# Two heads as one 48-row block in the recurrence, 128-row attention scores with the forget sums as a row sent by DMA, and alternating head products

## The reference

```
# branch a (rwkv): per head a 64x64 state S, over the 272 tokens
sa = S a_t
S  = S * w_t + sa b_t^T + v_t k_t^T
y_t = S r_t
# then a norm of each head, a bonus term, and a gate

# branch b (fox): q, k normed per head, c = cumsum(log_sigmoid(f)) per head
sc = q k^T / 8 + c[query] - c[key]       (causal)
out = softmax(sc) v
```

## Time and profile before

| | |
|---|---|
| median of three runs | 3304.73 us (3299.08 to 3321.63) |
| the profiled execution | 3333.08 us, its span 3331.0 us |
| mean granted TensorE clock of it | 0.955 |
| TensorE busy | 3198.3 us (96%) |
| DVE busy | 1728.7 us (52%) |
| ScalarE busy | 1240.5 us (37%) |
| HBM traffic | 145 GB/s over the span |

### The profile page before, as it was taken

How to read it: one execution, slowest core, us unless ns; L and a number is a source line. 1 busy time by engine, 2 the same in 40 slices (tenths; PEclk the granted TensorE clock), 3 DMA queues, 4 the chain that set the end, 5 groups by cost and what they waited for, 6 DMA issues and landing times.

```text
span 3331.0 us, 58202 instructions
## 1 busy us (share of the span) xinstructions
PE 3198.3 (96%) x24889; PEld 3018.6 (91%) x24889; DVE 1728.7 (52%) x2641; ACT 1240.5 (37%) x1824; POOL 61.3 (2%) x92
## 2 busy tenths in 40 slices
PE   7999889999999989979999999999999999999999
PEld 6999889999999989978878778778899999999999
DVE  5567565445554456454454444454465555555444
ACT  4354354333333444342222222333544333333343
POOL 0001000000000000000000000000000000000000
PEclk9999999999999999997897888999999999999999
DMA  5665445555555544542121111433354555555554
GB/s 199 199 170 144 137 142 177 188 180 186 187 179 188 187 154 147 174 123 55 52 68 49 45 40 52 126 102 90 122 180 167 180 186 188 180 187 183 185 188 139
DMA packets 369801, 484.93 MB, mean 146 GB/s; under 512 B 11847, under 2 KB 181142, under 8 KB 369638
## 3 DMA queue, kind: packets, MB, share of 16 engines
q1 hardware_dynamic: 362752, 471.55, 44.0%
q0 software_dynamic: 3600, 7.86, 0.8%
q10 hardware_dynamic: 3302, 3.39, 0.3%
HBM read 475.76 MB, written 7.01 MB: 145 GB/s over the span
## 4 chain that ended last, share of the span: by engine, by line
PE 89%; DVE 7%; ACT 3%; issue 1%; DMA 0%; DVEq 0%; SPq 0%; POOL 0%; ACTq 0%; POOLq 0%
PE psum L339 20%; PE psum L338 20%; PE psum L337 20%; PE psum L1683 7%; PE psum L468 5%; PE psum L472 4%; PE psum L470 4%; DVE w_lo L319 1%; DVE w_lo L455 1%; PE psum L1651 1%; ACT w_hi L310 1%; PE psum L2315 1%; DVE arena L1959 1%; PE psum L2314 1%; DVE arena L773 0%
## 5 line engine op out<-in xcount | busy, mean ns | idle before, releaser
L337 PE MATMUL psum<-act_hi,w_hi 128*128 128x256 f32 (+1 forms) x5840 | 1652.2, 283 | 61.7 <-DVE act_lo L864 18.1
L338 PE MATMUL psum<-act_lo,w_hi 128*128 128x256 f32 (+1 forms) x5840 | 1655.7, 284 | 0.0
L339 PE MATMUL psum<-act_hi,w_lo 128*128 128x256 f32 (+1 forms) x5840 | 1654.6, 283 | 0.0
L319 DVE TENSOR_TENSOR w_lo<-w_raw,w_hi 128x1024 fp32r<-128x1024 f32 x728 | 858.7, 1221 | 894.0 <-ACT w_hi L310 893.9
L310 ACT ACTIVATE w_hi<-w_raw 128x1024 fp32r<-128x1024 f32 x728 | 730.6, 1051 | 1207.6 <-PE psum L339 1207.6
L337 PEld LDWEIGHTS psum<-act_hi,w_hi 128*128 128x128 f32 x5840 | 1111.8, 190 | 68.6 <-issue 28.9
L339 PEld LDWEIGHTS psum<-act_hi,w_lo 128*128 128x128 f32 x5840 | 1113.1, 191 | 0.0
L338 PEld LDWEIGHTS psum<-act_lo,w_hi 128*128 128x128 f32 x5840 | 1104.8, 189 | 0.3
L468 PE MATMUL psum<-act_hi,w_hi 128*128 128x256 f32 (+1 forms) x1280 | 398.4, 311 | 2.5 <-DVE arena L1352 2.5
L470 PE MATMUL psum<-act_lo,w_hi 128*128 128x256 f32 (+1 forms) x1280 | 373.1, 291 | 0.0
L472 PE MATMUL psum<-act_hi,w_lo 128*128 128x256 f32 (+1 forms) x1280 | 372.8, 291 | 0.0
(11 more groups left out here) (374 smaller groups left out, 1672.1 us busy)
## 6 DMA issues: line engine op xcount, KB each, us to landing
w_raw<-w_in SPq DMA_DIRECT2D x128, 1024.0 KB, 5.5
w_raw<-w_down SPq DMA_DIRECT2D x88, 1024.0 KB, 5.1
w_raw<-w_gate_up SPq DMA_DIRECT2D x88, 1024.0 KB, 4.8
w_raw<-w_gate SPq DMA_DIRECT2D x44, 1024.0 KB, 5.0
w_raw<-w_up SPq DMA_DIRECT2D x44, 1024.0 KB, 5.1
w_raw<-w_out SPq DMA_DIRECT2D x16, 1024.0 KB, 5.2
w_raw<-w_o SPq DMA_DIRECT2D x16, 1024.0 KB, 5.1
w_raw<-w_branch_a SPq DMA_DIRECT2D x8, 1024.0 KB, 5.1
```

Of the source, the lines that this page charges most:

```text
L319: nc.vector.tensor_tensor(w_lo[:, s % 2, 2 * h:2 * h + 2, 0:wd], w_raw[:, s % RAW, 2 * h:2 * h + 2, 0:wd], w_hi[:, s % 2, 2 * h:2 * h + 2, ...
L337: pe.matmul(dst, w1, x1, start=first, stop=False, skip_group_check=True)
L338: pe.matmul(dst, w1, x0, start=False, stop=False, skip_group_check=True)
L339: mm = pe.matmul(dst, w0, x1, start=False, stop=stop and k == UNIT_K - 1, skip_group_check=True)
```

## The change

What is computed stays the same. In the recurrence, the 16-row blocks of the two heads are kept as one 48-row block (the first head in rows 0 to 15, the second in rows 32 to 47, zeros elsewhere, cleared once), and are multiplied once, with the second head's products. The three transposes of the 16 tokens become six products of 64 rows. The gram products go to other PSUM banks, DVE masks the half that the inversion needs first and the other half in two parts later, and DVE's filler slots are placed otherwise. The products x, y, state and s0 alternate between the heads.

In the attention, the q and k operands of each head have 128 rows: 64 with the head's values, one row of ones in q against the head's forget sums in k, zeros in the rest. POOL sends the forget sum rows from `c_neg` by two DMAs for each pair of heads. The scores are then one 128-row product. The products of `o` alternate between heads; the sums of squares of q and k go to two column groups of one bank, so that reciprocal, root and spread work on rows 0 to 15 and 32 to 47. The forget gate's logarithm is taken in the recurrence's groups 4 (DVE), 5 (ACT) and 6 (DVE).

```diff
+        PAIR = 32 + META
+        mh = [slice(32 * h, 32 * h + META) for h in range(2)]
...
-        tokm = place(3, P)
-        gm0 = place(2, 2 * META)
+        tokm = place(3, RHD)
+        gm0 = place(2, PAIR)
         inv_s = [place(4, P) for _ in range(6)]
-        inv_m = [place(2, META) for _ in range(6)]
+        inv_m = [place(PAIR) for _ in range(6)]
...
-                return psum[0:META, 2 * q + bank, 2 * P:2 * P + META]
-            return psum[:, 2 * (q // 2) + bank, (q % 2) * P:(q % 2 + 1) * P]
+                return psum[0:PAIR, 4 + bank, 2 * P:2 * P + PAIR]
+            return psum[:, 4 * (q // 2) + bank, (q % 2) * P:(q % 2 + 1) * P]
...
+                hs = [slice(h * RHD, (h + 1) * RHD) for h in range(2)]
                 for n, src in enumerate((bh[:, 0:META], kh[:, 0:META], zt(16 + j)[:, 0:META])):
-                    mm = pe.transpose(psum[0:META, 2, n * P:(n + 1) * P], src, ident)
+                    for h in range(2):
+                        mm = pe.matmul(psum[mh[h], 2, n * RHD:(n + 1) * RHD], src[hs[h]],
+                                       ident[hs[h], hs[h]], start=True, stop=True)
...
+                            o = psum[:, 2 * n + h, 2 * P * c:2 * P * (c + 1)].rearrange(
+                                "p (a t) -> p a t", a=2)
+                            pe.matmul(o[0:64], src[r, t0:t0 + 64], ar[r, :, t0:t0 + P],
...
-                    return f(h, True) if meta else last
+                    return f(h, True) if meta and h else last
...
-                for h in range(2):
-                    mm = pe.matmul(psum[0:META, 0, hs[h]], gm0[0:META, h, META:2 * META],
-                                   tokm[0:META, 2, hs[h]], start=True, stop=True)
-                mm.then_inc(*rp.did(("x0", j)))
+                pe.matmul(psum[0:PAIR, 0, 0:RHD], gm0[0:PAIR, 1], tokm[0:PAIR, 2], start=True, stop=True) \
+                    .then_inc(*rp.did(("x0", j)))
...
+                    y = [psum[hs[h], 4 + c, 0:P] for h in range(2)]
                     for h in range(2):
-                        o = psum[hs[h], 4 + c, 0:P]
-                        pe.matmul(o, us[:, h], gm[:, 2 * h + c, P:2 * P], start=True, stop=False)
-                        pe.matmul(o, vtok[:, hs[h]], gm[:, 2 * h + c, 3 * P:4 * P], start=False, stop=False)
-                        mm = pe.matmul(o, state_h[hs[h], :], ar[hs[h], 1, t], start=False, stop=True)
+                        pe.matmul(y[h], us[:, h], gm[:, 2 * h + c, P:2 * P], start=True, stop=False)
+                    for h in range(2):
+                        pe.matmul(y[h], vtok[:, hs[h]], gm[:, 2 * h + c, 3 * P:4 * P],
+                                  start=False, stop=False)
+                    for h in range(2):
+                        mm = pe.matmul(y[h], state_h[hs[h], :], ar[hs[h], 1, t], start=False, stop=True)
                     if c == 0:
...
+                if j == 5:
+                    fox_act_f()
...
+                def gram_mask(n, hs):
+
+                    q, c, k = slice(2 * hs[0], 2 * hs[-1] + 2), slice(2 * P * n, 2 * P * (n + 1)), 2 * len(hs)
+                    src = psum[:, 2 * n + hs[0]:2 * n + hs[-1] + 1, :]
+                    v.tensor_tensor(gm[0:64, q, c], src[0:64].rearrange("p h (c t) -> p (h c) t", c=2),
+                                    mask[0:64].unsqueeze(1).broadcast_to([64, k, 2 * P]), ALU.mult)
+                    late = lambda t: t[64:P].rearrange("p q (a t) -> p q a t", a=2)[:, :, :, 64:P]
+                    return v.tensor_tensor(late(gm[:, q, c]), late(src.rearrange("p h (c t) -> p (h c) t", c=2)),
+                                           mask[64:P].rearrange("p (a t) -> p a t", a=2)[:, :, 64:P]
+                                           .unsqueeze(1).broadcast_to([64, k, 2, 64]), ALU.mult)
+
+                gram_mask(0, [0, 1]).then_inc(*D_("gram"))
+                for h in heads:
+                    ins = v.tensor_tensor(gm0[mh[h], :, mh[h]],
+                                          psum[mh[h], 4, 0:2 * META].rearrange("p (n t) -> p n t", n=2),
+                                          mask[mh[h], mh[h]].unsqueeze(1).broadcast_to([META, 2, META]),
+                                          ALU.mult)
...
-                side(3)
                 for h in heads:
                     step("nt8", h, lambda s, p, n, t: TTn(s(0), p(0), t(T["lower8"]), ALU.mult),
                          PEA(("nt", h)))
                 for h in heads:
                     step("int8", h, lambda s, p, n, t: TTn(s(1), s(0), t(ident), ALU.add),
                          A_(("nt8", h)))
-                side(1)
+                gram_mask(1, [0])
+                side(2)
                 for h in heads:
                     step("p2", h, lambda s, p, n, t: v.tensor_copy(s(3), p(0)), PEA(("p2", h)))
                     step("ip2", h, lambda s, p, n, t: TTn(s(5), p(0), t(ident), ALU.add))
+                side(2)
                 for h in heads:
                     step("ip4", h, lambda s, p, n, t: TTn(s(3), p(0), t(ident), ALU.add),
                          PEA(("p4", h)))
+                gram_mask(1, [1])
                 for h in heads:
                     step("nm16", h, lambda s, p, n, t: TTn(s(2), n, t(T["join16"]), ALU.mult))
                 for h in heads:
...
+                if j in (4, 6):
+                    fox_dve_abs() if j == 4 else fox_dve_log()
...
+        C_ROW = (RHD, 0)
+        qn = [inv[:, 0:SEQ], tab[:, table_at["head_sum"][0]:table_at["head_center"][1]]]
+        kn = [scan_tab[:, 768:768 + TOK], sum_sq]
+        c_rows = sem("c_rows")
...
+        def fox_pool():
+
+            g = nc.gpsimd
+            g.wait_ge(*fd.after("ones"))
+            for j in range(8):
+                if j:
+                    g.wait_ge(*fp.after(("scores", j - 1)))
+                for h in range(2):
+                    n = 2 * j + h
+                    g.dma_start(kn[h][C_ROW[h]:C_ROW[h] + 1, 0:TOK], c_neg[n:n + 1]).then_inc(c_rows, 16)
+
...
+            for j in range(8):
+                for n, rows in enumerate((slice(0, 32), qk_rows[1])):
+                    at = 14 - 2 * j
+                    mm = pe.matmul(psum[rows, 0, 0:TOK],
+                                   T["half_to_row"][:, at:at + rows.stop - rows.start],
+                                   fsq[n][:, j], start=j == 0, stop=j == 7, skip_group_check=True)
...
-                    for n in range(2):
+                    for n, rows in enumerate(qk_rows):
                         for h in range(2):
+                            lane = rows.start + 2 * j + h
                             mm = pe.matmul(psum[h * RHD:(h + 1) * RHD, n, 0:TOK],
-                                           ident[0:LANES, 2 * j + h:2 * j + h + 1]
-                                           .broadcast_to([LANES, RHD]),
-                                           small2[0:LANES, n], start=True, stop=True)
+                                           ident[rows, lane:lane + 1].broadcast_to([LANES, RHD]),
+                                           rows_qk[rows], start=True, stop=True)
                     mm.then_inc(*fp.did(("spread", j)))
                     side(4)
                 if j > 0:
...
-                    pe.wait_ge(*fd.after(("kn", j)))
+                    pe.wait_ge(*fd.after(("kn1", j)))
+                    pe.wait_ge(c_rows, 32 * (j + 1))
                     for h in range(2):
-                        r = slice(h * RHD, (h + 1) * RHD)
-                        head = ident[0:LANES, 2 * j + h:2 * j + h + 1].broadcast_to([LANES, P])
                         for c, (o, n) in enumerate(((0, N1), (N1, N2))):
-                            out_ = psum[:, 4 + h, o:o + n]
-                            pe.matmul(out_, qn[r, c * P:(c + 1) * P], kn[r, 0:n], start=True, stop=False)
-                            mm = pe.matmul(out_, head, c_neg[0:LANES, 0:n], start=False, stop=True)
+                            mm = pe.matmul(psum[:, 4 + h, o:o + n], qn[h][:, c * P:(c + 1) * P],
+                                           kn[h][:, 0:n], start=True, stop=True)
...
+                hs = [slice(h * RHD, (h + 1) * RHD) for h in range(2)]
+                for h, r in enumerate(hs):
+                    pe.matmul(psum[r, 2, 0:SEQ], vtm[0:META, r], fwm[0:META, h], start=True, stop=False,
                               skip_group_check=True)
-                    pe.matmul(o[:, 0:SEQ], vt[:, 0, r], fwt[:, h, 0:SEQ], start=False, stop=False,
+                for h, r in enumerate(hs):
+                    pe.matmul(psum[r, 2, 0:SEQ], vt[:, 0, r], fwt[:, h, 0:SEQ], start=False, stop=False,
                               skip_group_check=True)
-                    mm = pe.matmul(o[:, P:SEQ], vt[:, 1, r], fwt[:, h, 256:384], start=False, stop=True,
-                                   skip_group_check=True)
+                for h, r in enumerate(hs):
+                    mm = pe.matmul(psum[r, 2, P:SEQ], vt[:, 1, r], fwt[:, h, 256:384], start=False,
```

(32 more changed lines are left out.)

146 lines of the change are left out of this document (69 added, 77 removed).

## The result

The changed kernel takes 3152.06 us (median of 4 runs, 3150.63 to 3154.46), the kernel before beside it 3303.15 (4 runs, 3299.08 to 3321.63). The ratio is 0.9533, with a 95% interval of 0.9496 to 0.9569. The forecast was 3175. The time lies inside the range of 3128 to 3240. It is 23 us under the forecast and 2 us above the band of rival 2, the clock high all through. The profiled execution of the changed kernel took 3150.63 us with a span of 3148.6, against a span of 3331.0 before: 182.4 us less.

The account below looks back on a forecast made before the run. TensorE, 89% of what ends last, was taken to bound the kernel. From 3333 us profiled, 46 (scan), 45 (fox attention) and 56 (clock) gave 3186, less 11 for run difference: 3175, range 3128 to 3240.

Parts of the forecast that it names:

- rival 2: Inversion blocks and attention: clock high all through, 83 us back, 3130 to 3150 us in the runs; chance 0.18.
- The clock term: Inversion blocks and attention: 48 of 66 us and 8 of 17 come back, 56 us in all, ends 0 and 83.
- Gram mask: Scan, ahead of the inversion: masking only the needed half first removes TensorE's wait, 1.3 us per group.
- Side(3): Scan, ahead of the masked transpose: DVE's filler slot leaves that place and the wait goes, 0.6 us per group.
- Inversion, net 1.2: Scan's inversion: nine fewer tiny products save 3.0 us per group, new waits for DVE take 1.0 and 0.8.
- Output products 2.7: Scan's y and x products: alternating heads overlaps column halves and saves shape changes, 2.7 us per group.
- toks, 0.5 as a cost: Scan's token transposes: three records become twelve 64-row ones, costing 0.3 us if heads overlap, 0.7 if not; 0.5 taken.
- The logarithm: Forget gate, attention's start: moving it into groups 4 to 6 removes a 4.2 us wait, plus 1.5 for late filler.
- From profile to runs: Whole kernel: runs lie 11 to 34 us below the profiled execution; 11 of the 28 taken off the forecast.
- 1: Inversion blocks: the clock falls as before, so the 56 us become 0, about 3225 us; chance 0.24.
- 3: Scan and attention: alternated pairs do not overlap and the clock stays unmended, about 3260 to 3280 us; chance 0.06.
- 4: Edited stretch: the low clock spreads into filler and the kernel gets slower, 3366 us in the runs; chance 0.03.

Follow-up runs that it names:

- e2: Changed kernel with DVE masking the whole gram product first and its side work ahead of the masked transpose again, restoring both old waits: 3181.95 us.
- e3: Changed kernel with nine extra 48x48 products per group in the inversion, making eighteen tiny products as before: 3170.52 us.
- e4: Changed kernel with the edits of e2 and e3 together, both old waits and eighteen tiny products per group: 3284.07 us.
- e5: Kernel before the change with the 16-row products of the inversion left out, old waits kept: 3238.46 us against 3302.32, ratio 0.9783.
- e8: Changed kernel with the attention's output products one head after the other again: 3161.99 us.
- e10: Changed kernel with DVE's two later half masks and first two filler slots moved into gaps further down: 3145.25 us.
- e11: e10 with the transposed inverse computed before the plain one in stages 16, 32 and 64, single products in the other PSUM bank: 3134.13 us.
- e6: Changed kernel with the scan's x, y, state and s0 products one head after the other again: 3173.79 us.

## Why the prediction was right, and where its sizes were off

The time lies in the stated range, and the list of what changes is right, but the forecast had the clock half mended and the runs show it wholly mended. That is rival 2, which had 0.18 against 0.49 for the forecast. The number is nearer than this step deserves, since 11 us that were taken off for another reason hide part of the miss.

**What bounds it** held: the time went where TensorE's work, waits and clock went, and DVE's added operations cost only where TensorE waited for them.

**The clock term was mis-sized.** "I take three of eight blocks low for two thirds of it": none was low. About 82 us came back instead of 56: all 66 of the blocks instead of 48, and 16 in the attention instead of 8. The step took the new wait ahead of p4 (1.05 on average) and the tiny products that are left for enough to keep the level down now and then. The runs show what was missing: e2 has longer waits and 9 tiny products, and recovers within a block; e3 has 18 and shorter waits, and never falls. It took long waits and 18 tiny products together (e4) to stay low, and the kernel before without the tiny ones (e5) did not. The change halved the one and took away the other. For the attention's 16 us the cause is not shown: e8 puts the outputs back in order and the grant stays 1.00, and neither the scores nor the spreads were put back. The prediction had both halves of this in rows 3 and 4, but weighed them as a chance.

**Gram mask**: 1.44 of wait gone, 2.3 us for the half, no new wait there; taken as 1.3. **Side(3)**: with the shape changes of the nt products TensorE's way from the first transposed block to the inversion fell from 2.58 us (1675.89 to 1678.47) to 1.60; 0.6 and part of 0.4 had been taken.

**Inversion, net 1.2**: the block fell from 21.1 to 20.5, so 0.6. The wait before p4 was met (8.4 in eight, 1.0 taken), and the later ones are 1.1 a group (3.2 + 5.7 in eight) where 0.8 was taken, so waits inside the blocks rose from 3.2 to 17.3 us, 1.8 a block. Nine tiny products less are 3.0 by the prediction's price, but the nine that are left cost 0.41 instead of 0.33 each, so 2.3 is saved and 0.6 remains. e10 and e11 show that 1.8 more a block was there to be had.

**Output products 2.7**: y 0.93 twice and x 0.5 twice are 2.9; in the runs 2.7 (e6, which puts s0 and the state in order as well). The mechanism, equal shapes in different column halves overlap when they are neighbours, is the one that the order of e6 takes away.

**toks, 0.5 as a cost**: the twelve records take 0.44 to the filler; one after the other they would take 12 x 0.056 = 0.67 (an estimate, 64 columns by the 0.112 of 128) without any shape change. They start in pairs 0.005 to 0.007 us apart, so heads overlap. From the first transpose to the filler it is 0.98 us (1750.73 to 1751.71) where it was 0.68 (1732.03 to 1732.71), so the cost is the 0.3. Here too the state product of y, L1760: four records of 128 columns in 0.36 us, where four at 0.112 are 0.45 without any shape change, and its pairs start 0.006 us apart. Both pairs have different rows of the array and one PSUM bank. The Trainium skill, "TensorEngine Tiling (Array Packing)", Restrictions and Gotchas, says that different row tiles cannot access the same PSUM bank at once; this trace contradicts it for these pairs, whose outputs lie in different partitions, and the sum by the rows was the one to keep. Pairs whose outputs share partitions are in no run.

**Scan in all**: 46 taken, about 50 measured. **Attention**: 45 taken, 44 and about 9 at the logarithm measured. Scores 3.1 a pair (2.6 taken: it is the second end, every shape change gone), outputs 1.35 (1.36), squares 3.66 (3.6), the spread 1.13 to 0.69 (0.3 taken, about 0.45). The logarithm: 8 in the runs, with 1.0 of it the square root's wait (5.7 and 1.3 taken); the low clock behind it was not in that sum.

**From profile to runs**: 11 taken off because some blocks are high in the usual run. With none low there is nothing left to differ: 3150.63 profiled against a median of 3152.06. On the profiled basis the forecast was 3186, 35 over: 26 by the clock, 4 by the scan and 8 by the attention with its logarithm, less 2 that the tail grew. The 11, and the 1.5 by which the profiled run lies under the median, bring that to the 23 between 3175 and 3152.

**Costs put at nothing**: DVE's two more multiplies a pair and POOL's row transfers cost nothing, as TensorE has no idle time there. The transfers of 1.1 KB land 3.1 and 3.3 us after their issue in the median of each buffer (5.7 at most), by the DMA issues of the changed kernel:

```profile
tab<-small POOLq DMA_DIRECT2D x8, 1.1 KB, 3.3
```

Of the rivals, 1 (the clock falls as before) is what e4 shows; 2 (high all through) is what happened; 3 is refuted by e6 and e8, each of which takes overlap away and pays for it; 4 did not occur, no filler of the edited stretch ran low. What stays open: why two of eight blocks before, and one in e4, stay high after the same waits, and why the number differs from run to run.

## What to carry to other kernels

When a stretch has two durations for the same work, take the low clock apart into what makes it fall and what keeps it from recovering, and put a price on each alone and on both: here 30, 18 and 132 us. Products that can share the array must be neighbours in TensorE's order and of one tile shape; the distance between the starts of single records shows whether they do (0.006 us against 0.11). Work moved out of one wait should go behind the step whose successor is latest, found by listing, for each stage, which of DVE's replies TensorE takes first.

## What the runs showed of the hardware that was not expected

- The clock's price is not additive. Waits of 15.5 + 4.7 us cost 30, nine more tiny products a block 18, both 132.
- A product that computes next to nothing is not free: a 48x48 one between 128x128 ones adds 0.41 us at 2.4 GHz (e3), a 16x16 one 0.33 (the kernel before).
- Two row tiles write one PSUM bank side by side when their outputs lie in different partitions (L1760 and L1644 above, 0.006 us from start to start).
